# mLSTM and S5 hybrid step on one core: whole-chunk opening, gate products on four column groups, and a new order in head 0

## The chip, the cores and the metric

The kernel runs on one core of one Trainium2 chip. The metric is the device time of one execution in microseconds. A core has a tensor engine (TensorE, PE in the profile; PEld is its weight load), a vector engine (VectorE, DVE), a scalar engine (ScalarE, ACT), GpSimd (POOL) and a queue engine (SyncE, SP). Each takes its own instructions in order, and they meet at semaphores. Products go to PSUM, eight banks of 512 fp32 columns, here the tensors G (four banks, in pairs A and B) and Q (four banks).

## The reference, cut to what matters

One step of a layer for 512 prompt tokens and 8 sample tokens together (520 columns), in fp32:

```python
h = rmsnorm(x, g_mix)                       # x * rsqrt(mean(x*x) + eps) * g
proj = h @ w_in + b_in                      # -> q, k, v, o, ig, fg, u, gl
hA = mlstm_mixer(q, k, v, ig, log_sigmoid(fg), C0, n0, m0)   # 4 heads
yA = (sigmoid(o) * head_norm(hA) * g_hn) @ w_a
yS = s5_mixer(u, ...)                       # complex diagonal scan, abar = exp(dt*A)
mix = (sigmoid(gA) * yA + sigmoid(gB) * yB) @ w_out
x = x + mix
x = x + (silu(hf @ w_ff1) * (hf @ w_ff3)) @ w_ff2            # hf = rmsnorm(x)
```

abar needs exp, cos and sin of dt*A, and for the sine the argument is brought into one turn first ("range reduction"). The gate logits ig and fg are 4 + 4 columns of w_in.

## The kernel before, in words

**Tiles.** Activations lie with features on partitions: X, HH, HL are [128, 8, 520]. The columns are worked as two halves, 256 and 264. A dense product is exact to fp32 by splitting both factors into a high part (fp32r, rounded) and a low part: ACT copies the raw weights to w_high (`high`, L439), DVE subtracts to get w_low (`low`, L1051), and `product` (L1580) sums high*high, high*low and low*high, per 128-row block one product of each kind for either half. A weight tile ("unit") is 128 x 1024; units go through a ring of three slots, and SP loads the next one into a slot when its w_low is made.

**Opening.** SP loads x in four pieces and then units 0 (gates), 1 (u) and 2 (first k tile). ACT squares x (L458), DVE adds the squares in pairs (`add_squares`, L1104), TensorE multiplies the four sums by ones, which leaves the sum in every row (L1592). ACT takes the root, DVE the reciprocal `rx` of all 256 or 264 columns (L1130), and scales x with it (L1149) into one of two buffers; ACT rounds that to HH, DVE subtracts to HL (L1135). This goes in two passes, first half, then second. TensorE follows block by block: gates (L1603, three terms, 64 columns wide), u and k (L1608), then the low terms (L1613, L1618, L1621), and then unit 3 by `product`. In between DVE does the range reduction (L1119 to L1121), and after the last h_low the powers of abar (L1158 to L1165), with w_low of unit 3 between the first squaring and the second. POOL waits for all scaled x before it loads c_samples and builds the S5 tables.

**Head 0.** After v, the gate columns are turned (L1632), DVE forms the state-major input matrix (bbar, L1216 to L1221) and then copies the gate columns (gates_ready). ACT makes exp weights (L594), POOL masks them, TensorE makes scores (L1715), numerators (L1725), the prompt's new state (L1765, `c_prompt`, into pair A, which o_gate has read), the S5 kernels (L1743) and the S5 steps (L1756, into pair B). The steps need BAQ, a spread copy of BA by parity: 16 pieces by ACT (L439, baq_act) and 16 by DVE (L1277, baq_dve). ACT takes the steps to s_state (x_used) and the prompt state to CO (co_ready); two dense units follow, on B behind x_used and on A behind co_ready. DVE runs the scan by doubling (L1351 to L1354), for which POOL computes powers (scan_known). Heads 1 to 3 are alike, then come gates, merge, output, feed-forward.

Each engine's order is written out by hand; nothing is planned by a program.

## Time and profile before

| | us |
|---|---|
| median of 3 runs | 962.22 (961.78 to 962.44) |
| the profiled execution's own time | 961.61 |
| its span, first to last instruction | 959.9 |
| TensorE busy | 935.0 |
| DVE busy | 541.4 |
| ACT busy | 441.1 |
| POOL busy | 192.6 |

Busy times are of the profiled execution. Matmuls overlap in the array, so a row's last record adds a tail to the group's time. "Idle before" names what ended an engine's waiting; the waits view sums those.

### The profile page before, as it was taken

Reading aid. Unit: us, or ns where it says so; the run is one execution under the profiler, and the core shown is the slowest. Engines: PE = TensorE matmul, PEld = TensorE weight load, DVE = VectorE, ACT = ScalarE, POOL = GpSimd, SP = SyncE. Lnnn points to the kernel's source line nnn. Section 1 sums busy time; section 2 is a strip of 40 time slices with the busy share of each in tenths; the row PEclk is TensorE's granted clock in tenths of the full one; section 3 lists DMA queues with packets and bytes.
Section 4 is the critical chain, followed back from the end, with each engine's and each line's share of the span. In section 5 each row is a group of like instructions: output and inputs, shape, how many; then the busy total and the mean of one; then the engine's idle time right before and its main releaser. Section 6 shows DMA issues by size and latency. Waiting matters only on the chain.

```text
span 959.9 us, 21395 instructions
## 1 busy us (share of the span) xinstructions
PE 935.0 (97%) x8874; PEld 912.4 (95%) x8874; DVE 541.4 (56%) x939; ACT 441.1 (46%) x734; POOL 192.6 (20%) x357
## 2 busy tenths in 40 slices
PE   4999999999999999999999999999999999999997
PEld 4898899999999999999999999999999999999997
DVE  6998893794594496753344656444444444333334
ACT  5468629828837847633233434332342342222221
POOL 3397876731823021000000000000000000000000
PEclk8999999999999999999999999999999999999998
DMA  7432136263244334633323222223222223333312
GB/s 277 170 98 102 49 119 254 100 242 122 90 162 159 112 137 148 220 111 110 104 96 109 88 88 89 87 87 105 92 87 88 87 89 98 98 91 108 95 58 89
DMA packets 28077, 113.23 MB, mean 118 GB/s; under 512 B 3524, under 2 KB 5620, under 8 KB 26088
## 3 DMA queue, kind: packets, MB, share of 16 engines
q1 hardware_dynamic: 23472, 80.80, 26.7%
q0 software_dynamic: 2736, 24.13, 6.6%
q10 hardware_dynamic: 1800, 7.31, 2.0%
q8 instruction: 53, 0.87, 0.3%
...
## 4 chain that ended last, share of the span: by engine, by line
PE 86%; DVE 8%; POOL 3%; issue 1%; ACT 1%; DMA 1%; ACTq 0%; DVEq 0%; POOLq 0%
PE G L1580 69%; PE G L1657 4%; PE Q L1580 2%; PE G L1925 2%; PE Q L1715 1%; PE Q L1725 1%; POOL pool_tmp L798 1%; DVE w_low L1051 1%; PE G L1765 1%; PE Q L1689 1%; DVE x_scaled L1149 1%; DMA a_params<-apar 1%; PE G L1756 1%; PE Q L1795 1%; DVE h_low L1135 0%
## 5 line engine op out<-in xcount | busy, mean ns | idle before, releaser
L439 ACT ACTIVATE w_high<-raw 128x1024 fp32r<-128x1024 f32 (+1 forms) x147 | 154.7, 1057 | 287.8 <-PE G L1580 273.0
L1051 DVE TENSOR_TENSOR w_low<-raw,w_high 128x1024 fp32r<-128x1024 f32 x146 | 180.8, 1241 | 174.2 <-ACT w_high L439 173.6
L1580 PE MATMUL G<-h_high,w_high 128*128 128x256 f32 x1344 | 272.8, 284 | 1.7 <-DVE x_residual L1499 0.9
L1580 PE MATMUL G<-h_low,w_high 128*128 128x256 f32 x1344 | 270.9, 283 | 0.8 <-issue 0.8
L1580 PE MATMUL G<-h_high,w_low 128*128 128x256 f32 x1344 | 270.7, 283 | 0.0
L1580 PEld LDWEIGHTS G<-h_high,w_high 128*128 128x128 f32 x1344 | 208.4, 188 | 4.0 <-issue 1.6
L1580 PEld LDWEIGHTS G<-h_high,w_low 128*128 128x128 f32 x1344 | 208.3, 188 | 0.9 <-issue 0.9
L1580 PEld LDWEIGHTS G<-h_low,w_high 128*128 128x128 f32 x1344 | 208.4, 188 | 0.0
L1580 PE MATMUL G<-hidden_low,w_high 128*128 128x256 f32 (+1 forms) x308 | 62.1, 283 | 0.0
L1580 PE MATMUL G<-hidden_high,w_high 128*128 128x256 f32 (+1 forms) x308 | 62.1, 283 | 0.0
L1580 PE MATMUL G<-hidden_high,w_low 128*128 128x256 f32 (+1 forms) x308 | 61.8, 281 | 0.0
L439 ACT ACTIVATE b_abar_by_step<-b_abar,parity 32x256 f32<-32x256 f32 x112 | 50.6, 498 | 0.7
L1580 PEld LDWEIGHTS G<-hidden_low,w_high 128*128 128x128 f32 x308 | 47.9, 188 | 0.0
L1580 PEld LDWEIGHTS G<-hidden_high,w_low 128*128 128x128 f32 x308 | 47.7, 188 | 0.0
L1580 PEld LDWEIGHTS G<-hidden_high,w_high 128*128 128x128 f32 x308 | 47.5, 188 | 0.0
L1525 DVE TENSOR_TENSOR ff_b<-G,ffn_rstd 128x256 f32<-128x256 f32 x22 | 9.3, 425 | 63.7 <-PE G L1580 63.7
L957 POOL TENSOR_TENSOR unused_p<-unused_p 128x1 f32<-128x1 f32 x29 | 12.8, 444 | 142.4 <-ACT c_prompt_out L439 29.7
L439 ACT ACTIVATE hidden_high<-ff_b 128x520 f32 (+1 forms) x22 | 14.1, 639 | 43.9 <-DVE ff_b L1531 43.9
L1324 DVE SCALAR_TENSOR_TENSOR c_samples<-v_spread,sample_small,c_samples 128x256 f32<-128x256 f32 x64 | 32.0, 576 | 0.0
L1534 DVE TENSOR_TENSOR hidden_low<-ff_b,hidden_high 128x520 f32 (+1 forms) x22 | 15.4, 700 | 20.0 <-ACT hidden_high L439 20.0
L1657 PE MATMUL G<-h_low,w_high 128*128 128x256 f32 (+1 forms) x128 | 25.8, 283 | 0.0
L1657 PE MATMUL G<-h_high,w_low 128*128 128x256 f32 (+1 forms) x128 | 25.8, 283 | 0.0
...
## 6 DMA issues: line engine op xcount, KB each, us to landing
raw<-wst SPq DMA_DIRECT2D x147, 512.0 KB, 3.6
...
x_residual<-xt POOLq DMA_DIRECT2D x1, 2080.0 KB, 10.4
...
```

What stands on the lines that cost most here:

```text
L439: return act.activation(out, in_, ACT.Copy, **kw)
L798: own.do(tt(o, a, b, ALU.mult))
L957: return tt(junk_p[:, g:g + 1], junk_p[:, 0:1], junk_p[:, 0:1], ALU.mult)
L1051: tt(WL[n.slot()][:], raw[n.slot()][:], WH[n.slot()][:].bitcast(F32), ALU.subtract).then_inc(w_lo, 1)
L1149: stt(xg[k % 2][:, c0_:c0_ + w], X[:, k, c0_:c0_ + w], g_mix[:, k:k + 1], rx[:, c0_:c0_ + w], ALU.mult, ALU.mult).then_inc(xg_ready, 1)
L1324: last = stt(CS[:, b, d, :], vB[:, b, :], kw[:, d, b:b + 1], CS[:, b, d, :], ALU.mult, ALU.add)
L1534: tt(HIDL[:, ff, :], ff_b[0][:].unsqueeze(1), HIDH[:, ff, :].bitcast(F32), ALU.subtract).then_inc(hidl_ready, 1)
L1580: last = mm(o, w[slot][:, c], h[:, k, c0_:c0_ + width], start=start and x == 0 and t == 0, stop=stop and x == n - 1 and t == 2)
L1657: last = mm(o, w[sl][:, wc], h[:, k, c0_:c0_ + width], start=k == 0 and t == 0, stop=k == KC - 1 and t == 2)
L1689: last = mm(Q[32 * jj:32 * jj + 32, 3, NB * t:NB * t + NB], CA[:, t + 1, c, 32 * jj:32 * jj + 32], S[:, c, jj, 0:NB], start=False, stop=t ...
L1715: last = mm(Q[:, q_bank, q_off:q_off + SEQ - P * j], kT[:, e, P * j:P * j + P], qT[:, e, P * j:SEQ], start=e == 0, stop=e == NE - 1)
L1925: last = mm(G[:, B + half, 0:w], wt[n.plus(j).slot()][:, P * x:P * x + P], h[:, k, c0_:c0_ + w], start=j == 0 and x == 0 and t == 0, stop= ...
```

## The change

- The opening works on all 520 columns at once. The squares are summed on DVE to one tile; TensorE sums it by token into five columns, so root and reciprocal are of 128 x 5, and a product with an identity (`ident_early`, made by POOL) spreads the reciprocal back over the partitions into Q. Eight buffers hold scaled x.
- Six products of ones with a cleared tile stand ahead of the sums on TensorE.
- The gate products take the scaled x itself and raw fp32 weights (`gate_w`), 32 columns wide, each (half, gate) on a column group of its own: output rows 0, 32, 64, 96. Unit 0 has no w_low any more.
- Range reduction moves to POOL; the apar load moves from ACT's queue to SP's, between x and the weights; the sines come after all of HH and after w_high of unit 3; w_low of unit 3 comes after both squarings.
- Before the loop of heads, gates_ready comes ahead of bbar on DVE, and POOL does two products of BA's last level ahead of the mask.
- In head 0 the steps go to pair A and the prompt state to pair B; CO is taken ahead of s_state; the second half of ACT's spreads comes after o_gate, pad_ca before it; DVE's spreads become eight of twice the size; scale_tokens comes ahead of the wait for scan_known; two w_low come behind V.

```diff
+        def prompt_pair(h):
+            return B if h == 0 else A
 
         def norm_bank(h, e):
             return e
...
-        xg = [sb(f"x_scaled{k}", [P, T], at=at_wt + 2112 * (2 + k)) for k in range(2)]
-        rx = sb("x_rstd", [P, T], at=at_wt + 2112 * 4)
+        xg = [sb(f"x_scaled{k}", [P, T], at=at_wt + 2112 * (k + k // 4) if k < 6 else at_kt + 2112 * (k - 6)) for k in range(KC)]
+        gate_w = sb("gate_weights", [P, KC, 64], at=at_kt + 2112 * 2)
...
+            sp.dma_start(par[:], apar).then_inc(par_in, 16)
             for n in range(RING):
...
-            act.dma_start(par[:], apar).then_inc(par_in, 16)
             for k in range(KC):
                 act.wait_ge(x_in[k // 2], 16)
                 act.activation(x_sq[:, k, :], X[:, k, :], ACT.Square).then_inc(sq_ready, 1)
-                if k == 1:
-                    act.wait_ge(par_in, 16)
-                    act.activation(par[:, 2, :], par[:, 2, :], ACT.Exp).then_inc(s5_dt, 1)
+            act.wait_ge(par_in, 16)
+            act.activation(par[:, 2, :], par[:, 2, :], ACT.Exp).then_inc(s5_dt, 1)
             act.wait_ge(s5_arg, 1)
...
-            copy(gate_cols(WH[0][:]), gate_cols(raw[0][:])).then_inc(w_hi, 1)
-            for half, (c0_, w) in enumerate(HALVES):
-                act.wait_ge(sq_summed, half + 1)
-                act.activation(rx[:, c0_:c0_ + w], Q[:, 2 + half, 0:w], ACT.Sqrt, bias=eps[:, 0:1], scale=1.0 / D).then_inc(rx_root, 1)
+            copy(gate_w[:], gate_cols(raw[0][:])).then_inc(w_hi, 1)
+            act.wait_ge(sq_summed, 1)
+            act.activation(rx[:, 0:SC + 1], G[:, B + 1, 0:SC + 1], ACT.Sqrt, bias=eps[:, 0:1], scale=1.0 / D).then_inc(rx_root, 1)
...
-            for half, (c0_, w) in enumerate(HALVES):
-                for k in range(KC):
-                    act.wait_ge(xg_ready, KC * half + k + 1)
-                    copy(HH[:, k, c0_:c0_ + w], xg[k % 2][:, c0_:c0_ + w]).then_inc(hh_ready, 1)
-                if half == 0:
-                    act.wait_ge(s5_ang, 1)
-                    act.activation(tp[4][:], tp[1][:], ACT.Sin).then_inc(s5_trig, 1)
-                    act.activation(tp[5][:], tp[3][:], ACT.Sin, bias=half_pi[:, 0:1], scale=-1.0).then_inc(s5_trig, 1)
-            after(At(0))
+            for k in range(KC):
+                act.wait_ge(xg_ready, k + 1)
+                copy(HH[:, k, :], xg[k][:]).then_inc(hh_ready, 1)
+            high(At(RING))
+            act.wait_ge(s5_ang, 1)
+            act.activation(tp[4][:], tp[1][:], ACT.Sin).then_inc(s5_trig, 1)
+            act.activation(tp[5][:], tp[3][:], ACT.Sin, bias=half_pi[:, 0:1], scale=-1.0).then_inc(s5_trig, 1)
...
-                            last = copy(BAQ[32 * q:32 * q + 32, jj, :, :, 64 * g:64 * g + 64], step_rows(jj, q),
+                            last = copy(spread_rows(jj, q)[:, :, g, :], step_rows(jj, q),
                                         scale=parity[32 * jj:32 * jj + 32, g:g + 1])
...
+                def take_prompt():
+                    act.wait_ge(c_done, h + 1)
+                    if h >= 1:
+                        act.wait_ge(co_out, 16 * h)
+                    for d in range(NE):
+                        last = copy(CO[:, d, :], G[:, prompt_pair(h) + d, 0:DH + 1])
+                    last.then_inc(co_ready, 1)
...
                     spread(0)
-                    spread(1).then_inc(baq_act, 1)
                     spread_samples()
...
+                if h == 0:
+                    pad_ca()
...
+                if h == 0:
+                    spread(1).then_inc(baq_act, 1)
                 high(n.plus(8 + RING))
                 if h == 0:
-                    pad_ca()
+                    take_prompt()
                 act.wait_ge(x_done, h + 1)
                 for c in range(2):
                     last = copy(S[:, c, :, 1:NCOL].rearrange("p (b j) n -> p b j n", b=2),
-                                G[:, B:B + 2, 0:288].rearrange("p b (j c n) -> p b j c n", j=2, c=2)[:, :, :, c, :])
+                                G[:, step_pair(h):step_pair(h) + 2, 0:288].rearrange("p b (j c n) -> p b j c n", j=2, c=2)[:, :, :, c, :])
                 last.then_inc(x_used, 1)
...
-                act.wait_ge(c_done, h + 1)
...
+                    take_prompt()
...
+            own.do(pool.memset(ident_early[:], 1.0))
+            own.do(pool.affine_select(out=ident_early[:], in_=ident_early[:], compare_op=ALU.is_ge, fill=0.0, base=0,
+                                      pattern=[[1, P]], channel_multiplier=-1))
+            pool.affine_select(out=ident_early[:], in_=ident_early[:], compare_op=ALU.is_ge, fill=0.0, base=0,
+                               pattern=[[-1, P]], channel_multiplier=1).then_inc(ident_made, 1)
...
+            pool.wait_ge(s5_turns, 1)
+            for c in (C1, C2, C3):
+                tsc(t[6], t[4], -c, ALU.mult)
+                add(t[1], t[1], t[6])
+            tsc(t[1], t[1], 3.1415925, ALU.min, -3.1415925, ALU.max)
+            tsc(t[3], t[1], 0.0, ALU.max, 2.0, ALU.mult)
+            tt(t[3], t[3], t[1], ALU.subtract).then_inc(s5_ang, 1)
...
-                    if i == 0 and w == 4:
-                        mask(0)
...
                     mul(f0, b, a_re)
                     mul(f1, b, a_im)
+                    if i == 0 and w == 4:
+                        mask(0)
                     sub(BA[:, w:2 * w, 0, :], g0[:, :, 0, :], g1[:, :, 1, :])
...
-            guard(xg_ready, 2 * KC)
+            guard(xg_ready, KC)
...
+                last = tt(x_sq[:, 2 * p, :], x_sq[:, 2 * p, :], x_sq[:, 2 * p + 1, :], ALU.add)
+                if p > 0:
+                    own.do(last)
+                    last = tt(x_sq[:, 0, :], x_sq[:, 0, :], x_sq[:, 2 * p, :], ALU.add)
+                if p < 3:
+                    own.do(last)
+                else:
+                    last.then_inc(sq_added, 1)
...
-            add_squares(0)
+            for p in range(4):
+                add_squares(p)
             dve.wait_ge(s5_dt, 1)
             own.do(tt(t[1], dt, ai, ALU.mult))
             tsc(t[4], t[1], 0.15915494309189535, ALU.mult)
             tsc(t[4], t[4], ROUND, ALU.add)
-            tsc(t[4], t[4], -ROUND, ALU.add)
...
+            ts(t[4], t[4], -ROUND, None, ALU.add).then_inc(s5_turns, 1)
+
+            dve.wait_ge(rx_root, 1)
+            dve.reciprocal(rx[:, 0:SC + 1], rx[:, 0:SC + 1]).then_inc(inverse_ready, 1)
             dve.wait_ge(w_hi, 1)
...
-            invert(0)
+            credit(w_lo)
+
+            def h_low(k):
+                dve.wait_ge(hh_ready, k + 1)
+                tt(HL[:, k, :], xg[k][:], HH[:, k, :].bitcast(F32), ALU.subtract).then_inc(hl_ready, 1)
+
+            low(At(1))
             dve.wait_ge(gb_in, 16)
-            for i in range(2 * KC):
-                k, (c0_, w) = i % KC, HALVES[i // KC]
-                if i == 5:
-                    low(At(1))
-                if i == KC:
-                    h_low(i - 1)
-                    invert(1)
+            dve.wait_ge(inverse_spread, 1)
+            for k in range(KC):
+                stt(xg[k][:], X[:, k, :], g_mix[:, k:k + 1], rx_all, ALU.mult, ALU.mult).then_inc(xg_ready, 1)
+                if k >= 1:
+                    h_low(k - 1)
+                if k == 3:
                     low(At(2))
-                if i >= 2:
-                    dve.wait_ge(hl_ready, i - 1)
-                stt(xg[k % 2][:, c0_:c0_ + w], X[:, k, c0_:c0_ + w], g_mix[:, k:k + 1], rx[:, c0_:c0_ + w], ALU.mult, ALU.mult).then_inc(xg_ready, 1)
-                if i not in (0, KC):
-                    h_low(i - 1)
-            h_low(2 * KC - 1)
+            h_low(KC - 1)
...
-            low(At(RING))
             k = 1
             square(a_pow[:, 0, k + 1, :], a_pow[:, 1, k + 1, :], a_pow[:, 0, k, :], a_pow[:, 1, k, :], 272)
             credit(pow_ready)
+            low(At(RING))
             low(At(N_MIX + RING))
...
+            own.do(dve.tensor_copy(bg[64:100, :], bg[0:36, :]))
+            for half, (c0_, w) in enumerate(HALVES):
+                r = 64 * half
+                own.add(ts(ig[:, c0_:c0_ + w], G[r:r + 4, A + half, 0:w], bg[r:r + 4, 0:1], None, ALU.add))
+                own.add(ts(fg[:, c0_:c0_ + w], G[r + 32:r + 36, A + half, 0:w], bg[r + 32:r + 36, 1:2], None, ALU.add))
...
+            own.settle()
+            dve.wait_ge(cols_done, 1)
...
+            dve.memset(V[:, :, DH:DH + 1], 1.0).then_inc(gates_ready, 1)
+            dve.wait_ge(gates_ready, 1)
+
             dve.wait_ge(f_ready, 1)
...
+                if h >= 1:
+                    low(n.plus(5 + RING))
+                    low(n.plus(6 + RING))
                 dve.wait_ge(w_ready, h + 1)
...
+                if h == 0:
+                    low(n.plus(5 + RING))
+                    low(n.plus(6 + RING))
...
-                            for g in range(2):
-                                last = ts(BAQ[32 * q:32 * q + 32, jj, :, :, 64 * g:64 * g + 64], step_rows(jj, q),
-                                          parity[32 * jj:32 * jj + 32, g:g + 1], None, ALU.mult)
+                            last = tt(spread_rows(jj, q), bcast(step_rows(jj, q), 2, [32, 2, 2, P]),
+                                      parity[32 * jj:32 * jj + 32, :].unsqueeze(1).unsqueeze(3).broadcast_to([32, 2, 2, P]), ALU.mult)
                     last.then_inc(baq_dve, 1)
...
+                    scale_tokens()
                     dve.wait_ge(scan_known, 1)
...
+                    if h >= 1:
+                        scale_tokens()
                     take_u(h + 1)
...
-            for p in range(4):
-                pe.wait_ge(sq_added, p + 1)
+            pe.wait_ge(uq_clear, 1)
+            for x in range(6):
+                mm(G[:, A, 0:512], ones[:], UQ[:].rearrange("p j h n -> p (j h n)")[:, 0:512], start=True, stop=True)
+            pe.wait_ge(sq_added, 1)
+            for i in range(SC + 1):
+                last = mm(G[:, B + 1, i:i + 1], x_sq[:, 0, tokens_in(i)], ones[:, 0:1], start=i == 0, stop=True, skip_group_check=True)
+            last.then_inc(sq_summed, 1)
+            pe.wait_ge(ident_made, 1)
+            pe.wait_ge(inverse_ready, 1)
+            for i in range(SC + 1):
+                part = ident_early[:] if i < SC else ident_early[:, P - NS:P]
+                last = mm(Q[:, 2 + i // SC, P * (i % SC):P * (i % SC) + part.shape[1]], rx[:, i:i + 1].broadcast_to([P, P]), part,
+                          start=True, stop=True)
+            last.then_inc(inverse_spread, 1)
+            for k in range(KC):
+                pe.wait_ge(xg_ready, k + 1)
+                if k == 0:
+                    pe.wait_ge(w_hi, 1)
                 for half, (c0_, w) in enumerate(HALVES):
...
+                    for g in range(2):
+                        r = 32 * (2 * half + g)
+                        last = mm(G[r:r + 32, A + half, 0:w], gate_w[:, k, 32 * g:32 * g + 32], xg[k][:, c0_:c0_ + w],
+                                  start=k == 0, stop=k == KC - 1, skip_group_check=True)
+                if k == KC - 1:
                     last.then_inc(unit_done, 1)
-                pe.wait_ge(w_lo, 2)
-                for k in range(KC):
-                    last = mm(G[:, B + half, 0:w], WL[1][:, P * k:P * k + P], HH[:, k, c], start=False, stop=k == KC - 1)
-                if half == 1:
-                    last.then_inc(unit_done, 1)
-                    for k in range(KC):
-                        for t, h in enumerate((HH, HL)):
-                            mm(Q[:, 1, 0:w], WH[2][:, P * k:P * k + P], h[:, k, c], start=k == 0 and t == 0, stop=False)
-                pe.wait_ge(w_lo, 3)
-                for k in range(KC):
-                    last = mm(Q[:, half, 0:w], WL[2][:, P * k:P * k + P], HH[:, k, c], start=False, stop=k == KC - 1)
+                pe.wait_ge(hl_ready, k + 1)
+                for u, out, terms in ((1, tiles(B), ((WH, HH), (WH, HL), (WL, HH))), (2, tiles(4), ((WH, HH), (WH, HL)))):
+                    if k == 0:
+                        pe.wait_ge(w_hi, u + 1)
+                        if u == 1:
+                            pe.wait_ge(w_lo, u + 1)
+                    for t, (wt, h) in enumerate(terms):
+                        for o, (c0_, w) in zip(out, HALVES):
+                            last = mm(o, wt[u][:, P * k:P * k + P], h[:, k, c0_:c0_ + w], start=k == 0 and t == 0, stop=u == 1 and k == KC - 1 and t == 2)
+                    if u == 1 and k == KC - 1:
+                        last.then_inc(unit_done, 1)
+            pe.wait_ge(w_lo, 3)
+            for k in range(KC):
+                for o, (c0_, w) in zip(tiles(4), HALVES):
+                    last = mm(o, WL[2][:, P * k:P * k + P], HH[:, k, c0_:c0_ + w], start=False, stop=k == KC - 1)
             last.then_inc(unit_done, 1)
             unit(At(N_MIX + 2), HH, HL, 6)
...
+                    if h == 0:
+                        pe.wait_ge(o_ready, 2)
                     pe.wait_ge(baq_act, h + 1)
                     pe.wait_ge(baq_dve, 1)
                     for jj in range(PAIRS):
                         for c in range(2):
-                            bank, at = B + jj // 2, 144 * (jj % 2) + 72 * c
+                            bank, at = step_pair(h) + jj // 2, 144 * (jj % 2) + 72 * c
                             for half, w in ((1, NB + NS), (0, NB)):
                                 for r in range(0, P, 32):
-                                    last = mm(G[r:r + 32, bank, at:at + w], BAQ[:, jj, c, 1 - half, r:r + 32], UQ[:, jj, half, 0:w],
+                                    last = mm(G[r:r + 32, bank, at:at + w], BAQ[:, jj, 1 - half, r // 64, c, r % 64:r % 64 + 32], UQ[:, jj, half, 0:w],
                                               start=half == 1, stop=half == 0)
...
                     pe.wait_ge(ks_ready, h + 1)
-                    pe.wait_ge(o_ready, 2 * h + 2)
+                    if h >= 1:
+                        pe.wait_ge(o_ready, 2 * h + 2)
                     for d in range(NE):
                         for j in range(SC):
-                            last = mm(G[:, A + d, 0:DH + 1], KS[:, j, P * d:P * d + P], V[:, j, :], start=j == 0, stop=j == SC - 1)
+                            last = mm(G[:, prompt_pair(h) + d, 0:DH + 1], KS[:, j, P * d:P * d + P], V[:, j, :], start=j == 0, stop=j == SC - 1)
                     last.then_inc(c_done, 1)
...
-                pe.wait_ge(x_used, h + 1)
+                pe.wait_ge(co_ready if h == 0 else x_used, h + 1)
                 unit(n.plus(9), HH, HL, B)
-                pe.wait_ge(co_ready, h + 1)
+                pe.wait_ge(x_used if h == 0 else co_ready, h + 1)
                 unit(n.plus(10), HH, HL, A)
```

## Rows read from the trace of the kernel before

**Rows 1.** The page: busy us of each engine, and one group, busy us, mean ns.

```profile
PE 935.0 (97%) x8874; PEld 912.4 (95%) x8874; DVE 541.4 (56%) x939; ACT 441.1 (46%) x734; POOL 192.6 (20%) x357
...
L439 ACT ACTIVATE w_high<-raw 128x1024 fp32r<-128x1024 f32 (+1 forms) x147 | 154.7, 1057 | 287.8 <-PE G L1580 273.0
```

**Rows 2.** Waits of TensorE, whole run: engine, line, releaser: us in total, times, longest.

```profile
PE Q L1592 <- DVE x_sq L1104: 8.7, 2, 6.8
PE G L1603 <- DVE h_low L1135: 4.1, 2, 3.3
PE G L1765 <- ACT o_gate L638: 1.4, 1, 1.4
PE Q L1580 <- DVE w_low L1051: 1.2, 1, 1.2
...
PE G L1580 <- issue: 0.8, 1, 0.8
PE G L1580 <- ACT s_state L439: 0.8, 1, 0.8
```

**Rows 3.** Timeline of TensorE: start us, us, engine, line, operation, out<-in, groups.

```profile
39.88 1.12 PE L1621 MATMUL Q<-h_high,w_low 128*128 128x264 f32 x8
...
84.03 4.51 PE L1725 MATMUL Q<-V,attn_weights 128*128 128x257 f32 x20
...
118.95 1.96 PE L1795 MATMUL Q<-c_samples,qT 128*32 128x256 f32 x32
...
952.87 1.42 PE L1913 MATMUL Q<-ident_late,root_columns 128*128 128x128 f32 x6 [0.66 <-DVE root_columns L1558]
```

**Rows 4.** Windows, TensorE: stretch, length, busy (x records), granted clock, DMA share, GB/s.

```profile
22.00:24.00 2.00, 2.00 (x11) 0.50 0.43 74
24.00:26.00 2.00, 2.00 (x19) 0.98 0.47 188
```

**Rows 5.** Timeline of ACT in the opening, start us, us, engine, line, operation, out<-in, waits in brackets.

```profile
7.49 0.43 ACT L461 ACTIVATE a_params<-a_params 128x272 f32<-128x272 f32 x1 [1.48 <-DMA a_params<-apar]
7.82 3.25 ACT L458 ACTIVATE x_sq<-x_tokens 128x520 f32<-128x520 f32 x6
...
11.41 1.28 ACT L465 ACT_TABLE_LOAD   x1
...
26.36 0.51 ACT L481 ACTIVATE s_setup<-s_setup,half_pi 128x272 f32<-128x272 f32 x1
```

**Rows 6.** Groups of DVE by form, 0 to 36 us: busy us, mean ns | idle.

```profile
L1149 DVE SCALAR_TENSOR_TENSOR x_scaled<-x_tokens,gains_biases,x_rstd 128x264 f32<-128x264 f32 x8 | 3.9, 493 | 0.2
...
L1135 DVE TENSOR_TENSOR h_low<-x_scaled,h_high 128x256 fp32r<-128x256 f32 x8 | 3.4, 421 | 0.2
L1104 DVE TENSOR_TENSOR x_sq<-x_sq 128x520 f32<-128x520 f32 x4 | 2.6, 698 | 4.4 <-ACT x_sq L458 4.3
L1051 DVE TENSOR_TENSOR w_low<-raw,w_high 128x1024 fp32r<-128x1024 f32 x2 | 2.4, 1222 | 0.0
```

**Rows 7.** Timeline of POOL in the opening.

```profile
8.00 1.01 POOL L824 TENSOR_TENSOR s_setup<-a_params 128x272 f32<-128x272 f32 x1 [2.63 <-ACT a_params L461]
...
39.66 0.92 POOL L807 TENSOR_SCALAR c_packed<-c_packed 128x256 f32<-128x256 f32 x1
```

**Rows 8.** Timeline of DVE in the opening.

```profile
15.27 1.75 DVE L1130 RECIPROCAL x_rstd<-x_rstd 128x256 f32<-128x256 f32 x1 [0.60 <-ACT x_rstd L470]
...
38.89 0.98 DVE L1163 TENSOR_TENSOR s_setup<-abar_powers 128x272 f32<-128x272 f32 x1
...
42.43 0.44 DVE L1163 TENSOR_TENSOR s_setup<-abar_powers 128x272 f32<-128x272 f32 x1
```

**Rows 9.** Timeline of head 0: DVE, ACT and TensorE.

```profile
85.20 9.79 DVE L1277 TENSOR_SCALAR b_abar_by_step<-b_abar,parity 32x256 f32<-32x256 f32 x16 [0.63 <-POOL b_abar L912]
...
86.77 5.08 ACT L439 ACTIVATE b_abar_by_step<-b_abar,parity 32x256 f32<-32x256 f32 x11
...
96.56 3.72 PE L1765 MATMUL G<-V,k_scaled 128*128 128x257 f32 x16 [1.38 <-ACT o_gate L638]
```

92 lines of the change are left out of this document (25 added, 67 removed).

## The prediction

> **What bounds it now.** Start with the busy shares: TensorE is busy 97% of the span [rows 1], so the time is TensorE's work plus its idle time. The list of its waits says where that idle time is [rows 2]: 8.7 us before the sums of squares and 4.1 before the first products of scaled x, then 1.2 us before the third product (for w_low), 1.4 us before the prompt sum of head 0 (for o_gate) and twice 0.8 us at the product behind it. All of these lie in the opening and in head 0, and nothing else in that list reaches a microsecond. So the change can earn only in the opening and in head 0, and what is earned there reaches the end unless the other engines fall behind.
>
> The marker for the opening is the start of the fourth weight tile's product. The last L1621 group ends at 39.88 + 1.12 = 41.0 [rows 3], and 1.2 us of waiting [rows 2] puts the start at 42.2 us. The clock is at 1.2 GHz in 22 to 24 us, and from 24 us on at 2.4 GHz [rows 4]; the record count nearly doubles from one window to the next.
>
> **The opening, step by step.**
> Squares. The apar load moves from ACT's queue behind x on SP's, ahead of the weights. ACT no longer stops 1.48 us for it between squares, nor spends 0.43 on its Exp there [rows 5]. Six squares ended at 7.82 + 3.25 = 11.1; they now end between 9.2 (1.9 less) and 11.1 (x lands no sooner). I take 10.0, since x was competing with apar. DVE adds seven times instead of four, 0.70 each [rows 6], but only two of them follow the last square: sum at 11.5.
> Root. ACT's own chain is longer: Exp 0.43 [rows 5], POOL's product 1.01 [rows 7], another Exp of 0.43, table load 1.28 [rows 5], the copy of half a tile of gate weights 0.6 (a whole one is 1.06, [rows 1]): 10.0 + 3.8, with hand-overs 13.9; the root of five columns about 0.3. So the sums on TensorE (five one-column products) hide, and so do the six products on ones: twelve records of 512 columns, at L1725's 0.225 for 257 columns at the full clock [rows 3], cost 0.9 each at half of it; even if all run so, from 1.8 us on, they end at 12.6, when ACT is still busy for more than a microsecond. Root done 14.2. The reciprocal falls from 1.75 (and another in the second half) to 0.2 [rows 8]. Spreading it back costs TensorE, from the end of the kernel, 1.42 us for two and a bit tiles at the low clock [rows 3], so 2.2 for four and a bit: 16.6. DVE meanwhile does w_low of tile 1, 1.22 [rows 6], which waits for ACT's copy of 1.06 [rows 1]: done at 16.5 too. First scaled x starts about where it did before (17.0).
> Scaling. Before, sixteen half tiles at 0.49 + 0.42 [rows 6], a reciprocal of 1.8 and two w_low. Now eight whole ones: 0.68 + 0.67 (0.70 for 520 columns, [rows 6]), cadence 1.35 us, plus one w_low between: 2 x 0.68 + 8 x 0.67 + 6 x 0.68 + 1.2 = 12.0, ideal end 29.
> POOL. What lies against that: range reduction moves from DVE to POOL, nine operations of about 0.9 [rows 7], from about 13.5 to 23, just when DVE subtracts. The same DVE operation L1163 took 0.98 us with POOL busy and 0.44 with POOL idle [rows 8]. Bounds for the five two-input operations that meet it: 0 to 5 x 0.54 = 2.7, hardly less than nothing; I take 1.5 to 2, mostly met. End of the last h_low 30.5.
> The Trainium skill (SBUF — State Buffer, Who interferes with whom) says that a DVE instruction with two SBUF inputs and a GpSimd instruction that reads SBUF lock each other out for a whole instruction; rows 8 agree in size, and by that rule the full 2.7 us would be paid and the sum would be about 3.7.
> Powers. ACT now splits tile 3 (1.06) before the sines, loads their table (1.28) and does both (0.9, at 0.51 with the overlap, [rows 5]): 29.8 + 3.2 = 33.0. DVE waits for them, then two products and both squarings (ten operations of 0.44 at most alone, 4.4, and 0.54 more for each that POOL meets; POOL then has few long ones left, and I take 5.0) and only then w_low of tile 3: 33.0 + 5.0 + 1.2 = 39.2. Before, that w_low ended at 42.2.
> TensorE. Gates were 48 records of 0.12 (rows 3: L1621, eight in 1.12 with a tail of 0.28). Now 32 products of 32 columns in fp32, two records each. L1795 is the same form on four column groups: 32 records in 1.96 us, so eight in 0.5, and with the drain on both sides I take 0.75 per block. A block is 0.75 + 10 x 0.12 = 1.95 us; the first two run partly at the low clock. From the first h_low at 19.5: about 4.7 for those, 6 x 1.95, then 16 x 0.12: end at 37.8. It waits 1.4 us for w_low, as before. **Opening: 42.2 to 39.2, 3.0 us.**
> The Trainium skill (TensorEngine Tiling (Array Packing), Key Properties) says that changing the tiling mode drains the array. The block changes it twice, and the 0.25 us added to L1795's pace is what I allow for that; with none the sum is the same, since it lies under the 1.4 us wait.
>
> **Head 0.** The gates_ready part now precedes the bbar products on DVE, and POOL forms two products before the mask; both move the mask to about 4 us earlier, so scores and V stay ahead of TensorE. POOL gets its powers from DVE just ahead of tile 3's w_low, so at least 3 us earlier, and scale_tokens ahead of scan_known keeps DVE's scan ahead of the token transposes. None of this was a TensorE wait; I cost it at nothing.
> The prompt sum (96.56 before, 3.72 long, [rows 9]) goes to pair B and no longer waits for o_gate: minus 1.4. KS is needed, and ACT delivers it earlier because only half of its sixteen spreads of 0.46 (11 in 5.08, [rows 9]) come ahead of k_scaled. The unit behind goes to the pair that CO frees, not the one that s_state frees: minus 0.8. The second 0.8 is "issue", I leave it.
> New waits: the other eight spreads now stand behind o_gate on ACT, 3.7 us, so from o_gate at 93.3 baq_act comes at 97. TensorE starts c_prompt at 96.6 - 1.4 - 3.0 = 92.2 and is through it at 95.9, and through the kernels (16 records of L1795's kind, 1.1) at 97.0. On DVE sixteen spreads in 9.8 us [rows 9] become eight of twice the size with two tensor inputs: 8 x 0.65 = 5 to 8 x 1.3 = 10.4; then w_low and the numerators, which the kernels wait for: num_used 93 to 97.5 where TensorE asks at 96. I charge 0.5. **Head 0: 2.2 - 0.5 = 1.7 us.**
>
> Sum: 4.7 us. The profiled execution took 961.61 (span 959.9), 0.6 under the median of 962.22. 961.61 - 4.7 = 956.9; on the median's scale 957.5, and I give 957.3.
>
> **Rivals.**
> A: TensorE becomes the opening's bound. If POOL does not hold DVE, w_low of tile 3 is done at 37.2 and TensorE ends at 37.5: 4.7 us, both head 0 waits and the issue gap go, 3.0: 954.2. For: the h_low steps of before ran beside POOL only once. Against: rows 8.
> B: the opening earns, head 0 does not: baq_act or num_used take the place of o_gate and s_state. 3.0 - 0.2 gives 959.2; with contention at its upper end, 959.9.
> C, the other side: the four column groups take turns between full-width products. Then eight records cost 0.225 each, as full-width fp32 does (L1725: 20 in 4.51, [rows 3]): 1.8 us per block where I count 0.5, 8 x 1.3 = 10.4, and tile 3's product starts at 48.2. That is 6.0 later, less 2.2: 965.8. It decides from 0.9 us more per block. Against: L1795 plainly overlaps.
> D: it does little, within 0.2% (1.9 us, about what a measurement of this kernel tells from none): a later DVE stall in head 0 or 1 takes back what the opening gave. About 961.
>
> **How the numbers follow.** Forecast 0.50 (955.5 to 959), A 0.22, B 0.17, D 0.06, C 0.05. The range takes in A, the forecast and B with its upper end: 953.2 to 960.6. Faster by over 0.2%: forecast, A and B, 0.89; same 0.07; slower 0.04.
>
> **What would show it.** Tile 3's product near 39.2 with a w_low wait before it; h_low cadence 1.35 us, and longer while POOL runs; eight gate records in about 0.5 us; no o_gate or s_state wait in head 0, but perhaps one for b_abar_by_step or numerators. I am wrong if gate records follow each other at 0.2 us, if the h_low chain ends later than 33, or if TensorE's waits after 100 us grow by over 2 us.

## The result, and the profile after

The changed kernel takes 963.59 us (median of 20 runs, 960.82 to 964.64), the kernel before, run beside it on the same chip, 961.98 (20 runs). The ratio is 1.0015, with a 95% interval of 1.0009 to 1.0021: slower by 1.6 us where 4.7 us of gain were forecast. The profiled execution took 964.36, its span is 962.6.

The opening gained nearly what was predicted, and head 0 lost more than twice that. The page and the waits of TensorE show the balance; they answer to [rows 1, 2]. First the page's busy times with the group of w_high, then the waits (line, releaser: us in total, times, longest):

```profile
PE 941.0 (98%) x8906; PEld 912.6 (95%) x8906; DVE 532.7 (55%) x913; ACT 439.2 (46%) x725; POOL 199.6 (21%) x369
...
L454 ACT ACTIVATE w_high<-raw 128x1024 fp32r<-128x1024 f32 x146 | 154.1, 1059 | 292.7 <-PE G L1606 275.2
```

```profile
PE G L1791 <- ACT b_abar_by_step L454: 3.6, 1, 3.6
PE G L1620 <- DVE x_sq L1138: 3.6, 1, 3.6
PE G L1617 <- DVE u_by_step L1125: 1.8, 1, 1.8
PE Q L1862 <- ACT attn_weights L702: 1.7, 1, 1.7
PE G L1606 <- DVE s_out L1102: 0.9, 1, 0.9
PE G L1636 <- DVE x_scaled L1166: 0.9, 1, 0.9
```

The waits of the opening shrank (8.7 + 4.1 became 3.6 + 1.8 + 0.9 and a few of less), but part of that time is now filled with work without use: the six cleared products take 6.9 us (1.77 to 8.69). The waits for o_gate and s_state are gone, and one of 3.6 us for b_abar_by_step has come at the state products. Behind it stand 0.9 for s_out and 1.7 for the attention's weights. TensorE is also busy for 6 us more, 3.9 of it up to the fourth tile's product (the cleared products, less what the opening saves) and 2.9 in head 0, where part of its work ran slower.

**The opening.** TensorE's timeline, against [rows 3]:

```profile
1.77 6.92 PE L1617 MATMUL G<-u_by_step,ones 128*128 128x512 f32 x12 [1.77 <-DVE u_by_step L1125]
12.25 2.30 PE L1620 MATMUL G<-ones,x_sq 128*128 128x1 f32 x10 [3.57 <-DVE x_sq L1138]
15.22 2.27 PE L1626 MATMUL Q<-ident_early,x_rstd 128*128 128x128 f32 x10 [0.67 <-DVE x_rstd L1154]
18.42 1.11 PE L1636 MATMUL G<-x_scaled,gate_weights 128*32 128x256 f32 x8 [0.93 <-DVE x_scaled L1166]
...
25.89 0.65 PE L1636 MATMUL G<-x_scaled,gate_weights 128*32 128x256 f32 x8
...
27.85 0.65 PE L1636 MATMUL G<-x_scaled,gate_weights 128*32 128x256 f32 x8
...
37.69 2.09 PE L1654 MATMUL Q<-h_high,w_low 128*128 128x256 f32 x16
39.62 0.40 PE L1606 MATMUL Q<-h_high,w_high 128*128 128x256 f32 x2
```

The fourth tile's product starts at 39.62 in place of 42.2. From the third block on a block takes 27.85 - 25.89 = 1.96 us, but the first two take 7.5 together (18.42 to 25.89). The windows (against [rows 4]: stretch, length, busy with records of TensorE, its weight loads, DVE, ACT and POOL, granted clock, DMA share, GB/s) show them at 1.2 GHz until about 25 us (0.50 is 1.2 GHz, 1.00 is 2.4), and two later stretches partly at it too:

```profile
20.00:22.00 2.00, 1.66 (x7) 1.66 (x8) 2.00 (x4) 0.64 (x1) 1.83 (x3) 0.50 0.92 381
22.00:24.00 2.00, 2.00 (x14) 0.93 (x12) 2.00 (x3) 0.64 (x1) 2.00 (x3) 0.50 0.65 264
24.00:26.00 2.00, 2.00 (x14) 1.86 (x18) 2.00 (x4) 0.64 (x1) 1.70 (x3) 0.67 0.51 30
100.00:104.00 4.00, 3.17 (x120) 3.20 (x124) 2.24 (x4) 2.18 (x5) 3.54 (x11) 0.57 0.01 4
136.00:142.00 6.00, 5.65 (x34) 5.66 (x35) 5.86 (x11) 1.32 (x3) 0.27 (x1) 0.72 0.97 346
```

On the other engines the opening goes as drawn up; these lines answer to [rows 5 to 8] (ACT, DVE by form, the range reduction now on POOL, w_low of tile 3 on DVE):

```profile
31.73 0.43 ACT L491 ACTIVATE s_setup<-s_setup 128x272 f32<-128x272 f32 x1
```

```profile
L1160 DVE TENSOR_TENSOR h_low<-x_scaled,h_high 128x520 fp32r<-128x520 f32 x8 | 6.4, 795 | 0.1
L1166 DVE SCALAR_TENSOR_TENSOR x_scaled<-x_tokens,gains_biases,Q 128x520 f32<-128x520 f32 x8 | 5.9, 745 | 0.3 <-PE Q L1626 0.3
```

```profile
13.65 0.89 POOL L824 TENSOR_SCALAR s_setup<-s_setup 128x272 f32<-128x272 f32 x1 [2.74 <-DVE s_setup L1151]
...
21.85 0.77 POOL L855 TENSOR_TENSOR s_setup<-s_setup,s_setup 128x272 f32<-128x272 f32 x1
```

```profile
37.60 1.22 DVE L1082 TENSOR_TENSOR w_low<-raw,w_high 128x1024 fp32r<-128x1024 f32 x1
```

**Head 0.** ACT's timeline, against [rows 9]:

```profile
86.86 1.57 ACT L454 ACTIVATE k_scaled<-G,wk_columns 128x256 f32<-128x256 f32 x4
93.70 2.34 ACT L454 ACTIVATE c_abar<-c_abar_packed 64x1152 f32<-64x1152 f32 x2 [5.28 <-POOL c_abar_packed L960]
96.06 0.47 ACT L656 ACTIVATE o_gate<-G,head_params 128x256 f32<-128x256 f32 x1
...
96.93 3.65 ACT L454 ACTIVATE b_abar_by_step<-b_abar,parity 32x256 f32<-32x256 f32 x8
100.60 1.06 ACT L454 ACTIVATE w_high<-raw 128x1024 fp32r<-128x1024 f32 x1
```

k_scaled is ready at 88.4, long before TensorE asks (92.3). Then ACT stands idle for 5.28 us at pad_ca, which copies a table that POOL finishes only at 93.7; the gate, eight spreads and the rounding of tile 12 come behind it, and the last spread ends at 100.6. Tile 12 is the next weight tile; before, its rounding began 4.3 us earlier:

```profile
96.28 1.09 ACT L439 ACTIVATE w_high<-raw 128x1024 fp32r<-128x1024 f32 x1
```

TensorE stands in front of the state products from 97.2:

```profile
92.31 3.64 PE L1801 MATMUL G<-V,k_scaled 128*128 128x257 f32 x16
96.14 1.09 PE L1776 MATMUL Q<-c_abar,bbar_p 128*32 128x256 f32 x16 [0.18 <-issue]
100.83 3.50 PE L1791 MATMUL G<-u_by_step,b_abar_by_step 128*32 128x72 f32 x128 [3.60 <-ACT b_abar_by_step L454]
```

The state products take 3.5 us. Before, they took 2.1:

```profile
101.09 2.10 PE L1756 MATMUL G<-u_by_step,b_abar_by_step 128*32 128x72 f32 x128
```

DVE waits 6.57 us for the rounding of tile 12, so its chain of c_samples, scan and s_out is late from there on, and TensorE meets that later as 0.9 and 1.7 us:

```profile
101.76 1.24 DVE L1082 TENSOR_TENSOR w_low<-raw,w_high 128x1024 fp32r<-128x1024 f32 x1 [6.57 <-ACT w_high L454]
```

Two distances separate the stages: the start of v's product in head 0 (**M0**), and of v's product in head 1 (**M1**). Before, M0 is 59.6 and M1 140.8; after, 56.9 and 144.2. So the opening gained 2.7, and the stretch M0 to M1 grew from 81.2 to 87.3, by 6.1 us. From M1 to the end both kernels take the same within 1 us (819.1 and 818.4). The question is what makes the 6.1.

### The profile page after: what moved, and what is told of

Its sections match the earlier page's. It is cut to its first block, busy times and chain, and to the rows that moved or that the text cites. A ratio compares the mean times of both kernels' runs of the same rounds, so it can differ in the third digit from the quotient of the medians.

```text
span 962.6 us, 21437 instructions
## 1 busy us (share of the span) xinstructions
PE 941.0 (98%) x8906; PEld 912.6 (95%) x8906; DVE 532.7 (55%) x913; ACT 439.2 (46%) x725; POOL 199.6 (21%) x369
## 4 chain that ended last, share of the span: by engine, by line
PE 91%; DVE 5%; POOL 2%; ACT 1%; issue 1%; DMA 0%; DVEq 0%; SPq 0%; POOLq 0%; ACTq 0%
PE G L1606 70%; PE G L1690 5%; PE Q L1606 3%; PE G L1961 2%; PE Q L1748 1%; PE Q L1758 1%; PE G L1801 1%; PE G L1648 1%; POOL pool_tmp L815 1%; PE Q L1722 1%; DVE c_samples L1348 1%; PE G L1791 1%; PE Q L1831 1%; DMA x_tokens<-xt 0%; PE G L1636 0%
## 5 line engine op out<-in xcount | busy, mean ns | idle before, releaser
L454 ACT ACTIVATE w_high<-raw 128x1024 fp32r<-128x1024 f32 x146 | 154.1, 1059 | 292.7 <-PE G L1606 275.2
L815 POOL TENSOR_TENSOR pool_tmp<-c_abar_packed,abar_tile 128x128 f32<-128x128 f32 (+2 forms) x32 | 26.7, 833 | 2.5
```

The lines of the kernel that those rows point to most:

```text
L454: return act.activation(out, in_, ACT.Copy, **kw)
L815: own.do(tt(o, a, b, ALU.mult))
```

## The experiments

Theories at the start. **T**: ACT's queue stands at pad_ca, ahead of the gate, the late spreads and the rounding. **U**: DVE's spreads with two tensor inputs slow POOL's table, so that pad_ca comes late. **V**: the swapped pairs and the new order of the products cost something by themselves. Every kernel below is the changed one with the edit shown, unless the text names another. The times are medians; M0 and M1 are those of the one profiled execution of each kernel.

**E1, ACT's second spreads back behind the first.**

```diff
                     spread(0)
+                    spread(1).then_inc(baq_act, 1)
                     spread_samples()
...
-                if h == 0:
-                    spread(1).then_inc(baq_act, 1)
                 high(n.plus(8 + RING))
```

> Edit: in head 0 ACT makes its second eight spreads right behind the first eight again, ahead of k_scaled, pad_ca and o_gate; all else as changed. Theory T (ACT's order is the cause: it stands at pad_ca until POOL's c_abar table is there at 93.7, and o_gate, eight spreads and the w_high behind them are late): the 3.6 us wait of TensorE for b_abar_by_step goes, the steps run at 2.4 GHz in 2.1 us instead of 3.5, w_high behind them is made near 97 instead of 100.6, the waits of 0.9 and 1.7 us later in head 0 go, and the time is 956 to 958. Rival U (the late table itself is the cause, since POOL is held by DVE's two-input spreads): the table stays at 93.7, most of the wait moves to the S5 kernels, 961 to 963. Rival V (the swapped pairs or the order of CO and s_state cost it): no change, 963.6.

Measured: 956.91 us (956.65 to 958.19), ratio to before 0.9948 (0.9936 to 0.9961). The wait at the state products is gone, M0 to M1 is 78.6. This one statement's place is worth 6.7 us, more than the whole loss. ACT still waits 1.59 us at pad_ca, which costs TensorE no wait there. The time is the one T gave, but E8 below will show that T had the reason only in part.

**E2, DVE's spreads as sixteen one-tensor multiplies again.**

```diff
-                            last = tt(spread_rows(jj, q), bcast(step_rows(jj, q), 2, [32, 2, 2, P]),
-                                      parity[32 * jj:32 * jj + 32, :].unsqueeze(1).unsqueeze(3).broadcast_to([32, 2, 2, P]), ALU.mult)
+                            for g in range(2):
+                                last = ts(spread_rows(jj, q)[:, :, g, :], step_rows(jj, q),
+                                          parity[32 * jj:32 * jj + 32, g:g + 1], None, ALU.mult)
```

> Edit: DVE's eight spreads with two tensor inputs become sixteen with one again; ACT's order stays as changed. U: POOL's build of the table takes 11.3 us as before instead of 15.9, it is ready near 89, before TensorE's unit ends, ACT does not stand at pad_ca, the wait for b_abar_by_step falls below 0.5 us, and the time is 957 to 959. T: the same for the table, but then o_gate at 92.3 and 3.7 us of spreads put baq_act at 97.0, wait 0 to 0.5. If instead the two-input form does not matter: table at 93.7 again, 963.6. V: no change.

Measured: 960.06 us (958.29 to 960.62), ratio 0.9976 (0.9967 to 0.9985). POOL's timeline of the table, first of the changed kernel, then of this one:

```profile
77.84 0.53 POOL L948 COPY c_abar_packed<-c_packed 128x64 f32<-128x64 f32 x2
...
85.59 2.82 POOL L815 TENSOR_TENSOR pool_tmp<-c_abar_packed,abar_tile 128x512 f32<-128x512 f32 x2
...
93.35 0.32 POOL L960 TENSOR_TENSOR c_abar_packed<-pool_tmp,pool_tmp 128x64 f32<-128x64 f32 x1
```

```profile
76.21 0.54 POOL L948 COPY c_abar_packed<-c_packed 128x64 f32<-128x64 f32 x2
...
82.98 2.16 POOL L815 TENSOR_TENSOR pool_tmp<-c_abar_packed,abar_tile 128x512 f32<-128x512 f32 x2
...
88.24 0.33 POOL L960 TENSOR_TENSOR c_abar_packed<-pool_tmp,pool_tmp 128x64 f32<-128x64 f32 x1
```

The table takes 12.4 us in place of 15.8, ACT's wait for it 1.81 in place of 5.28, TensorE's 0.4 in place of 3.6. U holds as a second cause: the spreads still stand behind the gate, but the gate comes earlier. U's 957 to 959 was missed by 1.1 us, and the trace, of the fastest of the ten runs (958.29), shows a wait of 2.1 us for s_out that U did not name. DVE's own spreads take 8.95 us in the two-input form. In the other they take 9.79 before [rows 9], 9.36 here and 8.6 in E4, so no saving on DVE is shown, against 3.4 us on POOL.

**E4, all edits inside head 0 undone, the new opening kept** (pairs, orders on ACT, DVE and TensorE, both spreads).

```diff
         def step_pair(h):
-            return A if h == 0 else B
+            return B
...
         def prompt_pair(h):
-            return B if h == 0 else A
+            return A
```

> Edit: the new opening with all edits inside head 0 undone (pairs, ACT's order, DVE's form, scale_tokens, w_low order); gates_ready and the mask stay where the change puts them. If opening and head 0 add up: the opening's 2.6 us stays, TensorE waits for o_gate 1.4 and s_state 0.8 as before, 959.4. V: 959.4 as well. If the opening gave nothing that lasts: 962.

Measured: 957.07 us (955.06 to 959.85), ratio 0.995 (0.9934 to 0.9965). The new opening with the old head 0 is 4.9 us faster than before, and 2.3 faster than expected. V finds nothing, since E1, with all of V's edits in place, takes the same. The o_gate wait (1.8) and the s_state wait (0.8) are back here, M0 to M1 is 80.4 against 78.6 in E1: the good part of the head 0 edits is 1.8 us, in one execution of each; the medians do not show it.

**E6, four products without use (fp32, 512 columns) in the hole ahead of the state products.**

```diff
                     pe.wait_ge(uq_ready, h + 1)
                     if h == 0:
+                        for x in range(4):
+                            mm(Q[:, 2, 0:512], ones[:], V[:, 0:2, 0:DH], start=True, stop=True)
+                    if h == 0:
```

> Edit: four more products of ones with V (512 columns, results unused) stand on TensorE between the S5 kernels and the steps of head 0, inside the 3.6 us hole; nothing else. It measures what the clock costs there. If the low clock in the steps comes from the hole: the fill is busy 3.5 us, the steps start when they did (100.8) and take 2.1 instead of 3.5 us at 2.4 GHz, the time falls by about 1.4 us to 962.2, and more if DVE's chain is not what TensorE waits for next. If the clock falls for another reason: steps 3.5 us, 963.6.

Measured: 963.85 us (961.43 to 965.48), ratio 1.0015 (1.0006 to 1.0024): nothing gained over the changed kernel, where 1.4 us were expected. TensorE's timeline:

```profile
95.10 3.70 PE L1784 MATMUL Q<-V,ones 128*128 128x512 f32 x8
98.73 2.10 PE L1794 MATMUL G<-u_by_step,b_abar_by_step 128*32 128x72 f32 x128
...
118.99 0.50 PE L1606 MATMUL G<-h_high,w_high 128*128 128x256 f32 x2 [2.30 <-DVE s_out L1102]
```

The state products took 2.1 us again, 1.4 less. The wait for s_out grew from 0.9 to 2.3, by the same 1.4, and behind that wait the granted clock fell (0.58 in 120 to 122 us, 0.57 in 122 to 124). M0 to M1 is 86.0 in this execution, 1.3 under the changed kernel's, because the wait for the attention's weights is 0.5 and not 1.7; the medians show nothing of it. So the low clock of the state products is not the cause of the loss: DVE's lateness behind the rounding of tile 12 holds TensorE in any case.

**E8, pad_ca back behind the rounding of tile 12.** It is T's own test.

```diff
                 last.then_inc(ks_ready, 1)
-                if h == 0:
-                    pad_ca()
...
                 high(n.plus(8 + RING))
                 if h == 0:
+                    pad_ca()
                     take_prompt()
```

> Everything of the changed kernel, with one move: in head 0 ScalarE's two copies of the c_abar table (pad_ca, 2.34 us) go back behind the second output gate, the late spreads and the rounding of tile 12, where they stood before the change. Theory T (ScalarE stands at pad_ca for GpSimd's table, 5.28 us idle to 93.7, with the gate, the spreads and the rounding queued behind it): ScalarE goes straight on from 88.4, its spreads end near 93 and not 100.6, the rounding of tile 12 near 94; the state products start near 97.5 without the wait of 3.6 us, and the time falls by 6 to 7 us to 956 to 958, as with the early spreads. Rival U (the damage is GpSimd's slowness under VectorE's two-input spreads): the c_abar copies still come only at 93.7 to 96.1, and the kernel products at 96.3, so nothing is lost by it for TensorE; U alone expects less than 2 us, 961.5 to 963. Rival V (swapped pairs, order of the products): no change, 963.6.

Measured: 963.07 us (960.26 to 964.25), ratio 1.001 (1.0001 to 1.0019). T falls, the prediction of 956 to 958 with it. M0 to M1 is 85.6. ACT's and TensorE's timelines say why:

```profile
90.71 0.47 ACT L654 ACTIVATE o_gate<-G,head_params 128x256 f32<-128x256 f32 x1 [4.09 <-PE G L1605]
...
91.58 3.65 ACT L454 ACTIVATE b_abar_by_step<-b_abar,parity 32x256 f32<-32x256 f32 x8
95.25 1.06 ACT L454 ACTIVATE w_high<-raw 128x1024 fp32r<-128x1024 f32 x1
96.21 2.32 ACT L454 ACTIVATE c_abar<-c_abar_packed 64x1152 f32<-64x1152 f32 x2
```

```profile
98.63 1.96 PE L1775 MATMUL Q<-c_abar,bbar_p 128*32 128x256 f32 x16 [4.48 <-issue]
```

ACT idles 4.09 us all the same, now for the gate's own input, TensorE's product, which ends at 90.5. Behind it stand gate, spreads, rounding and c_abar copies, 7.8 us in a row, and TensorE waits 4.48 at the kernel products for the last of them (the list calls it issue; they start 0.1 us after the copies end). V had expected this number (no change, 963.6), so E8 alone does not tell V from what follows; E4 had already spoken against V. The timelines give theory **T2**: ACT idles 4 to 5 us ahead of the second gate whatever is done; before the change the eight spreads filled that time, now they stand behind the gate.

**E11, only that edit.** The kernel of E4 with ACT's second spreads put behind the gate.

```diff
                     spread(0)
-                    spread(1).then_inc(baq_act, 1)
                     spread_samples()
...
+                if h == 0:
+                    spread(1).then_inc(baq_act, 1)
                 high(n.plus(8 + RING))
```

> The version with all head 0 edits undone (957.1: new opening, old products' order, old pairs, pad_ca behind the rounding), with one edit of the change put back alone: ScalarE's second eight spreads behind the second output gate. Theory T2, which takes the place of T since moving pad_ca back brought nothing (963.1): ScalarE idles 4 to 5 us ahead of the second gate in any case, because the gate waits for TensorE's product; the late spreads leave that idle time and stand behind the gate together with the rounding (1.06) and pad_ca (2.34), 7.9 us in all, and the kernel and state products wait for the last of them. It expects here: gate near 93.3, spreads to 97.8, rounding, c_abar copies done near 101, a wait of TensorE of 2 to 4 us ahead of the kernel products, and 960 to 962. Rival V (it takes the swapped pairs and the products' new order to lose): 957.1 as without it. Theory T as first stated (only with pad_ca ahead of the gate): 957.1 to 958.

Measured: 962.0 us (959.81 to 963.36), ratio 0.9994 (0.9985 to 1.0003). Against E4's 957.07 this is 4.9 us more, with the old pairs, the old order, one-tensor spreads and pad_ca in its old place, where V and T as first stated had both put it at 957.1 to 958. M0 to M1 is 85.2, against 80.4 in E4. ACT's idle time ahead of the gate is only 2.86 us here, under T2's 4 to 5. TensorE waits as T2 said:

```profile
100.56 1.96 PE L1768 MATMUL Q<-c_abar,bbar_p 128*32 128x256 f32 x16 [3.21 <-issue]
```

**E12, the second spreads between k_scaled and pad_ca.**

```diff
                 last.then_inc(ks_ready, 1)
                 if h == 0:
+                    spread(1).then_inc(baq_act, 1)
                     pad_ca()
...
-                if h == 0:
-                    spread(1).then_inc(baq_act, 1)
                 high(n.plus(8 + RING))
```

> The changed kernel with the second eight spreads of ScalarE between its k_scaled copies (end 88.4) and pad_ca, in the idle 5.28 us, and nothing else changed: k_scaled stays early, the spreads stay later than before. Theory T2 (the spreads must lie in ScalarE's idle time; how early in it is all one): they run 88.4 to 92.1, pad_ca follows at 93.7 as in the changed kernel, the gate at 96, the rounding of tile 12 at 97 and not 100.6; no wait at the state products; 956 to 958, as with the early spreads (956.9). A rival, that k_scaled's early end or the lateness of the spreads themselves (against VectorE's and GpSimd's work) does the harm: 960 or more.

Measured: 956.27 us (954.88 to 957.25), ratio 0.9934 (0.992 to 0.9947). ACT's timeline:

```profile
88.99 3.66 ACT L454 ACTIVATE b_abar_by_step<-b_abar,parity 32x256 f32<-32x256 f32 x8
94.25 2.34 ACT L454 ACTIVATE c_abar<-c_abar_packed 64x1152 f32<-64x1152 f32 x2 [1.60 <-POOL c_abar_packed L959]
```

The spreads lie in the idle time, k_scaled stays early (done at 89.0), and pad_ca still waits for POOL. M0 to M1 is 78.6, as in E1. All of the loss is gone, so T2 holds from both sides: E11 makes the loss with this edit alone, E12 removes it by this statement's place alone.

**E3 and E10, the rest of head 0.** E3 is E1 with E2's edit; E10 is E3 with pad_ca moved back as in E8.

```diff
+                    spread(1).then_inc(baq_act, 1)
                     spread_samples()
...
+                            for g in range(2):
+                                last = ts(spread_rows(jj, q)[:, :, g, :], step_rows(jj, q),
+                                          parity[32 * jj:32 * jj + 32, g:g + 1], None, ALU.mult)
```

> The changed kernel with both halves of the spreads as before: ScalarE's second sixteen right behind its first, and VectorE's sixteen one-tensor multiplies in place of eight two-input ones. Theory T with U (both ScalarE's order and GpSimd's slowed table count, each alone brought 6.7 and 3.5 us, but they remove the same hole): GpSimd's table comes near 90.5, ScalarE waits under 0.5 us for it in place of 1.59, the rounding of tile 12 starts near 95.5 and not 96.9, and the time is 955.5 to 957, at most 1.4 us under the run with the early spreads alone. If the two added up: 953.4. Rival V (the swapped pairs and the new order cost something by themselves): slower than with all head 0 edits undone, 957.1, by over 1 us.

```diff
                 high(n.plus(8 + RING))
                 if h == 0:
+                    pad_ca()
                     take_prompt()
```

> The version with both spreads as before (956.7), and pad_ca back behind the rounding of tile 12. T2: with the spreads in the idle time, gate 0.9 and rounding 1.1 come ahead of the c_abar copies, which end near 94.5 in place of 93; TensorE's kernel products wait 0 to 1 us for them, while VectorE's chain starts some 3 us earlier; 956 to 957.5, no more than 0.5 us from the run without. If pad_ca's place matters by itself, as T first had it, 954 to 955.

Measured: E3 956.71 us (954.74 to 958.2), ratio 0.9948; E10 956.38 (954.52 to 956.66), ratio 0.9933 (0.9919 to 0.9946). Both lie where they were expected. With the spreads in the idle time neither POOL's slow table nor pad_ca's place can be measured; the gains of E1 and E2 do not add.

**The opening's clock: E5, E7 and E9.** All have the spreads early. E5 drops the six cleared products, E7 makes them ten, E9 (on E3) has ten and fills two more gaps. The edits of E5, E7 and, beside E7's, E9:

```diff
-            for x in range(6):
-                mm(G[:, A, 0:512], ones[:], UQ[:].rearrange("p j h n -> p (j h n)")[:, 0:512], start=True, stop=True)
```

```diff
-            for x in range(6):
+            for x in range(10):
```

```diff
             last.then_inc(sq_summed, 1)
+            mm(G[:, A, 0:512], ones[:], UQ[:].rearrange("p j h n -> p (j h n)")[:, 0:512], start=True, stop=True)
...
             last.then_inc(inverse_spread, 1)
+            for x in range(2):
+                mm(G[:, A, 0:512], ones[:], UQ[:].rearrange("p j h n -> p (j h n)")[:, 0:512], start=True, stop=True)
```

> The version with the early spreads (956.9), without the six cleared products ahead of the sums. They end at 8.7 to 10.1 and the granted clock is 0.50 from 12 us on all the same in most profiles, so the theory that they bring nothing here expects 956.5 to 957.5 with the same stretches at half clock, the fourth tile's product still starting near 39.6. The rival, that they hold the clock up over part of the gate blocks (in two of the profiles it was back by 21 to 23 us and not by 25), expects the clock to come back later, 2 us or more lost at the opening and the same at the end: 958.5 to 960.

> The version with the early spreads (956.9), with ten cleared products in place of six, so that TensorE works to about 12.2 us where the squares' sum is ready (12.25). Theory W (TensorE's idle 3.5 us ahead of the sums lets the clock fall, and the two first gate blocks then run at half speed, 7.5 us for what takes 3.9): the sums take 1.27 us and not 2.30, the spread of the root about 1.2 and not 2.27, the first two gate blocks 4 to 5 us and not 7.5, the fourth tile's product starts near 36.5 and not 39.6, and the time falls by 2 to 3 us to 954 to 955. Rival X (one-column sums, the wait for the root and the spread hold TensorE too little, so that the clock falls by 16 whatever came before): the blocks still run at half clock, the gain is the sums' 1 us or nothing, 956 to 957. A loss (the sums queue behind the cleared products): 957.5.

> The version with both spreads as before (956.7), with ten cleared products and three more of the same kind that fill TensorE's idle time at the opening: one behind the sums, two behind the spread of the root. Theory W2 (the fall of the clock in the first gate blocks follows the idle 0.7 and 1.5 us and the light products before them): the clock stays at 1.00 to the end of the opening, the first blocks take 2.0 us each and not 3.5 to 4, the fourth tile's product starts 2 to 3 us earlier than in the slower profiles (39.6) and at or under the fastest (36.9), and the time is 954 to 955.5 with a spread of runs under 2 us. Rival X: it falls all the same, 956.5 to 957.5. Rival Y: VectorE's low parts pace the blocks (0.98 to 1.22 us each beside GpSimd, 0.9 to 0.7 for x_scaled), so that warm products only wait: 955.5 to 956.5.

Measured: E5 956.57 us (955.99 to 957.43), E7 958.07 (955.89 to 958.69), E9 955.49 (954.14 to 955.96), ratio 0.9927 (0.9913 to 0.994). The six products as the change has them bring nothing that can be measured. Ten hold the clock through the sums (1.17 us and not 2.30) and the spread of the root (1.25 and not 2.27), then it falls in the idle 1.5 us ahead of the first block, and the first blocks run slow, so W is wrong and X right about the blocks. E7's time lies above both of their ranges: the sums began at 13.0, 0.8 later, behind the cleared products, and its profiled execution took 822.0 from M1 to the end, where the others took 818.4 to 820.1. What made that is open. With the gaps filled (E9) the clock is 1.00 throughout the opening, the eight blocks and the low terms end at 35.8 in place of 39.8, and TensorE now waits for DVE:

```profile
20.00:22.00 2.00, 2.00 (x23) 1.44 (x26) 2.00 (x3) 0.64 (x1) 1.83 (x3) 1.00 0.96 393
```

```profile
33.73 2.10 PE L1657 MATMUL Q<-h_high,w_low 128*128 128x256 f32 x16
...
36.96 0.51 PE L1606 MATMUL Q<-h_high,w_high 128*128 128x256 f32 x2 [1.14 <-DVE w_low L1081]
```

E9 beats both kernels, 6.7 us under before. That it also beats E12 or E10 is not shown, since the intervals overlap; with E3, the same kernel without the fills, they overlap as well (0.9935 to 0.9962). W2 is right about the clock, and Y about what TensorE waits for then; the time, 955.49, lies on the border of the two. E3's profiled execution had the clock back by about 21 us without any fill and its fourth tile's product at 37.23, only 0.3 later than E9's 36.96: the fills remove the late return, which comes in some executions and not in others. And E9's execution gave 1.5 us back in head 0, where the clock fell to 0.56 and 0.59 in 128 to 132 us (M0 to M1 80.8, in E3 79.3).

## Why the prediction was wrong, point by point

**The step that failed** is the one called new waits: "the other eight spreads now stand behind o_gate on ACT, 3.7 us, so from o_gate at 93.3 baq_act comes at 97". It charged nothing for baq_act, since TensorE was to be through the kernels at 97.0 as well, and 0.5 us for the numerators. Put behind the gate alone (E11), the spreads cost 4.9 us. Three things were wrong in the step.
- It never asked what the spreads had covered. Before, ACT worked without a break from 86.8 [rows 9] to 99.6, and the second gate's input was there only at 95.2 (96.56 - 1.38). Taking 3.7 us out of the front part of a queue does not bring forward a gate that waits for TensorE's product. It opened an idle stretch (2.86 us in E11, 4.09 in E8, 5.28 in the changed kernel) and pushed 3.7 us into the one place of the queue where TensorE and DVE wait for all that follows.
- It left pad_ca out. The change puts it ahead of the gate, where it waits for POOL. The gate came at 96.06, not 93.3, and the spreads at 100.6, not 97. E8 shows that this was not the decisive error: in the other place it is late for the kernel products instead.
- It counted the wait and not who stood behind it. The rounding of tile 12 went from 96.3 to 100.6 (36.7 to 43.7 us behind M0), and DVE's chain with it.

In numbers: M0 to M1 was to shrink by 1.7 us and grew by 6.1. Of that, 1.4 is the state products at the low clock (3.5 for 2.1), 1.5 the later product at the low clock in 136 to 142 us (136.8 to 144.2, 7.4 for 5.9), and the rest is waiting: 3.6 + 0.9 + 1.7, less the 1.4, 0.8 and 0.8 that the edits removed, 3.2. E6 shows that the first 1.4 cannot be had back separately. Of the prediction's three signs of being wrong the last one came: TensorE's waits after 100 us, with the one that ended at 100.8, grew by 4.6 us.

**The opening** was forecast at 3.0 us by the fourth tile's product, and 2.6 came. Sum (12.2), root (14.9), first scaled x (17.6), last h_low (30.2), sines (32.6) and w_low of tile 3 (38.8) all came within 0.7 us of their steps, the spread of the root (17.5) within 0.9. TensorE's end did not: it was done with the low terms and began the fourth tile at 39.6, and not at 37.8. The first block's dense products came at 20.3 and not 19.5, and from there the two blocks that ran mostly at the low clock took 5.5 us (20.34 to 25.89) where I gave 4.7. So TensorE and not w_low set the start, 0.8 us behind w_low. In part the agreement is luck. The h_low chain began 0.6 late and took 12.6 us, not 12.0 plus the 1.5 to 2 that I added for POOL, and that surplus hid the late start. The block at full speed, 1.96 us, is as predicted (1.95), which disposes of rival C: the eight records of the column groups take 0.65. In ten profiled executions of kernels with the six cleared products M0 lies between 54.6 and 57.5: the clock comes back between 21 and 27 us, and that spread of 2.9 us is of the size by which the runs of one kernel differ. By M0 the opening is therefore worth 2.1 to 5.0 us, against the one execution of before (59.6). E4's median says 4.9, and in its execution 0.8 of the gain lies between M0 and M1.

**POOL's contention** was seen where it was priced, the opening (h_low at 1.22 and 0.98 us beside POOL, 0.68 to 0.74 otherwise, one of these, 0.72, beside POOL too). It came to 0.8 us there and not 1.5 to 2. It was missed among the squares, where the addition at 10.20 took 1.26 us and not 0.70 beside POOL's product of 0.76 at 10.15, which is most of the 0.7 us by which the sum was late. And it was missed in head 0, where the change itself brought the two-input form to DVE. The table started 4.7 us earlier against M0 than before (20.9 and 25.6 us behind it) and ended at the same distance, 36.8 and 36.9.

**The waits named** did go: no wait for o_gate or s_state is left. The reordering of mask, powers and scale_tokens, costed at nothing, cost nothing that E1 or E12 shows.

**Rival B** was the nearest: it had baq_act take the place of o_gate, but with head 0 at a loss of 0.2 us where M0 to M1 grew by 6.1.
